# Another order of columns in the three-part matmuls of a whole-model kernel, and six offsets for the weights' split tiles

## The reference

```
x = x + gate * hybrid_mixer(modulate(x))    # gated linear attention and three-way sparse attention
x = x + gate * swiglu(modulate(x))          # dense feed-forward
x = x + gate * mamba2_mixer(modulate(x))    # state-space layer
x = x + gate * moe_ffn(modulate(x))         # 8 experts, the best 2 for each token
x = rmsnorm(x, final_norm)
for layer in range(2):                      # dilated attention beside block-sparse attention
    x = hybrid_layer(x, c, cos, sin, ...)
```

## Time and profile before

| | |
|---|---|
| median of 3 runs | 2075.34 us (2073.47 to 2078.24) |
| the profiled execution | 2075.21 us, span 2073.4 us |
| TensorE matmuls, weight loads | 95% and 79% of the span busy |
| VectorE, ScalarE | 83% and 64% |
| mean granted TensorE clock | 0.982 of 2.4 GHz |
| moved by DMA | 560 MB, 270 GB/s on the mean |

### The profile page before, as it was taken

One profiled execution on the slowest core, in us unless ns is written; L12 is line 12 of the kernel. 1 busy time (PEld: TensorE's weight loads), 2 busy tenths in 40 slices (PEclk: granted clock), 3 DMA queues, 4 the chain that ended last, 5 costly groups with the idle time before them and its releaser, 6 DMA issues.

```text
span 2073.4 us, 28446 instructions
## 1 busy us (share of the span) xinstructions
PE 1975.6 (95%) x10316; PEld 1644.3 (79%) x10316; DVE 1725.3 (83%) x2440; ACT 1328.1 (64%) x1977; POOL 0.2 (0%) x4
## 2 busy tenths in 40 slices
PE   6998999989989999999999999999999998999997
PEld 5777889978877788788888878888888876767785
DVE  7798878768776698989989898998989988785764
ACT  4353534355564587788788787888878774554543
POOL 0000000000000000000000000000000000000000
PEclk9999999999999999999999999999999999999999
DMA  9856689846332298999999999999989994672630
GB/s 378 300 170 234 229 301 327 287 142 207 116 111 82 91 382 325 359 334 382 366 351 365 329 368 345 374 352 340 371 325 377 380 354 158 222 247 68 217 122 21
DMA packets 154211, 560.19 MB, mean 270 GB/s; under 512 B 17232, under 2 KB 17488, under 8 KB 153936
## 3 DMA queue, kind: packets, MB, share of 16 engines
q1 hardware_dynamic: 154064, 558.29, 74.1%
HBM read 557.18 MB, written 1.05 MB: 269 GB/s over the span
## 4 chain that ended last, share of the span: by engine, by line
PE 78%; DVE 12%; ACT 5%; issue 3%; DMA 2%; DVEq 0%; SPq 0%; ACTq 0%
PE ps L527 22%; PE ps L529 22%; PE ps L528 22%; PE ps L533 10%; DVE spl L516 3%; PE ps L537 3%; DVE macc L580 2%; ACT sph L504 2%; DMA ring<-in_hyb_w_in 1%; DVE arena L2169 1%; DMA ring<-in_dense_down 1%; ACT arena L771 1%; ACT arena L2135 0%; DVE hL L884 0%; ACT ps L890 0%
## 5 line engine op out<-in xcount | busy, mean ns | idle before, releaser
L504 ACT ACTIVATE sph<-ring 128x1024 fp32r<-128x1024 f32 x906 | 949.2, 1059 | 517.0 <-PE ps L529 332.8
L516 DVE TENSOR_TENSOR spl<-ring,sph 128x1024 fp32r<-128x1024 f32 x906 | 1078.2, 1219 | 241.5 <-ACT sph L504 229.0
L527 PE MATMUL ps<-sph,hH 128*128 128x512 f32 (+1 forms) x1296 | 522.6, 403 | 1.4 <-DVE hL L884 1.3
L529 PE MATMUL ps<-sph,hL 128*128 128x512 f32 (+1 forms) x1296 | 507.8, 392 | 0.0
L528 PE MATMUL ps<-spl,hH 128*128 128x512 f32 (+1 forms) x1296 | 506.9, 391 | 0.0
L529 PEld LDWEIGHTS ps<-sph,hL 128*128 128x128 f32 x1296 | 245.5, 189 | 52.6
L527 PEld LDWEIGHTS ps<-sph,hH 128*128 128x128 f32 x1296 | 246.4, 190 | 51.3 <-issue 3.8
L528 PEld LDWEIGHTS ps<-spl,hH 128*128 128x128 f32 x1296 | 246.4, 190 | 48.4 <-issue 1.0
L527 PE MATMUL ps<-sph,rH 128*128 128x512 f32 x664 | 269.1, 405 | 5.9 <-ACT arena L3123 2.3
L529 PE MATMUL ps<-sph,rL 128*128 128x512 f32 x664 | 259.9, 391 | 0.0
L528 PE MATMUL ps<-spl,rH 128*128 128x512 f32 x664 | 259.4, 391 | 0.0
(11 more groups left out here) (317 smaller groups left out, 1754.4 us busy)
## 6 DMA issues: line engine op xcount, KB each, us to landing
ring<-in_moe_gu SPq DMA_DIRECT2D x448, 512.0 KB, 5.4
ring<-in_moe_down SPq DMA_DIRECT2D x224, 512.0 KB, 5.3
ring<-in_mod SPq DMA_DIRECT2D x144, 512.0 KB, 5.0
ring<-in_w_in SPq DMA_DIRECT2D x64, 512.0 KB, 4.5
ring<-in_dense_gu SPq DMA_DIRECT2D x44, 512.0 KB, 5.3
ring<-in_ssm_w_in SPq DMA_DIRECT2D x40, 512.0 KB, 4.2
ring<-in_dense_down SPq DMA_DIRECT2D x22, 512.0 KB, 5.4
ring<-in_hyb_w_in SPq DMA_DIRECT2D x20, 512.0 KB, 5.9
```

What stands on the lines that cost most here:

```text
L504: a.activation(k.high[m % SPLITS][:, 0:w], raw[:, 0:w], ACT.Copy).then_inc(k.S.half_rounded, 1)
L516: v.tensor_tensor(k.low[m % SPLITS][:, 0:w], raw[:, 0:w], k.high[m % SPLITS][:, 0:w], ALU.subtract).then_inc(*k.tick(k.S.half_split, f"hal ...
L527: pe.matmul(out, a[0], b[0], start=start, stop=False, skip_group_check=True)
L529: return pe.matmul(out, a[1], b[0], start=False, stop=stop, skip_group_check=True)
```

## The change

The moving operand of `mm3`, and its result in PSUM in the same way, are walked in another order of columns when their number is a multiple of 256. The columns are seen as two halves of n groups of 16; the groups are taken from the last to the first, and from each the 16 columns of the first half and then those of the second. The result lands at the same places as before. The pairs `sph`, `spl` are set apart by pads, so that pair i begins LEADS[i] float32 columns (0, 64, 128, 192, 320, 448 bytes) further modulo 512 than `hH`. The pads make 448 bytes, which also shift all tiles behind them (`macc`, `mods`, `ring`, `arena` and others); a reserve for descriptors in SBUF is made smaller to have the room (no transfer here is started from GpSimd).

```diff
+LEADS = (0, 16, 32, 48, 80, 112)
...
-        self.high = [sb(f"sph{i}", [128, QUARTER], F32R) for i in range(SPLITS)]
-        self.low = [sb(f"spl{i}", [128, QUARTER], F32R) for i in range(SPLITS)]
+        self.high, self.low = [], []
+        for i, lead in enumerate(LEADS):
+            if (lead - LEADS[i - 1] if i else lead) % 128:
+                sb(f"pad{i}", [128, (lead - LEADS[i - 1] if i else lead) % 128])
+            self.high.append(sb(f"sph{i}", [128, QUARTER], F32R))
+            self.low.append(sb(f"spl{i}", [128, QUARTER], F32R))
...
+def paced(ap):
+
+    return ap.rearrange("p (j n i) -> p n j i", j=2, i=16)[:, ::-1] if ap.shape[1] % 256 == 0 else ap
+
+
 def mm3(pe, out, a, b, start, stop):
-    pe.matmul(out, a[0], b[0], start=start, stop=False, skip_group_check=True)
-    pe.matmul(out, a[0], b[1], start=False, stop=False, skip_group_check=True)
-    return pe.matmul(out, a[1], b[0], start=False, stop=stop, skip_group_check=True)
+    out, high, low = paced(out), paced(b[0]), paced(b[1])
+    pe.matmul(out, a[0], high, start=start, stop=False, skip_group_check=True)
+    pe.matmul(out, a[0], low, start=False, stop=False, skip_group_check=True)
+    return pe.matmul(out, a[1], high, start=False, stop=stop, skip_group_check=True)
...
-    nc = _bacc.Bacc("TRN2", target_bir_lowering=False, num_devices=1)
+    nc = _bacc.Bacc("TRN2", target_bir_lowering=False, num_devices=1, dynamic_dma_scratch_size=1024)
```

## The result

The changed kernel takes 2079.28 us (median of 20 runs, 2072.85 to 2085.06), the kernel before 2074.28 us in as many runs on the same chips (2068.16 to 2079.80). The ratio is 1.0024 with a 95% interval of 1.0014 to 1.0034: 5 us slower, between 2.9 and 7.1. The prediction said 50 us faster. Of its four cases none came out as told. The change is a little slower; the sign given for rival (c) did show (distances that depend on the buffer, over 230 ns in three of six, see the table further down), but not its 13 ns.

The account below looks back on a forecast made before the run. The distance between `mm3`'s starts was taken to bound the kernel. Saving 8.5 ns each, 27.1 us in the experts' stage and 22.8 outside, gave 2075.2 - 49.9 = 2025 us; own range 2000 to 2055, whole range 2000 to 2100.

Parts of the forecast that it names:

- rival (c): In `mm3`, streams kept at one place in some buffers: 13 ns a matmul lost, 2118 to 2162 us; chance 0.17.
- the prediction's own sum: Whole kernel: `mm3` matmuls by stage times 8.5 ns, 27.1 us kept in the experts' stage, 22.8 outside, together 49.9.
- The 71%: Outside the experts' stage: share of `mm3`'s start distances that the chain of waits holds, 463 of 648 us; 22.8 us saved.
- The surplus of 13 ns: In `mm3` at full clock: 13.3 ns per matmul over its columns' time, read as two read streams of TensorE meeting.
- Part (2): Six places of the pairs in SBUF: the distance of the two streams differs by buffer; some can still meet.
- rival (b): In `mm3`, the surplus is the swap of the weights, not a meeting: saving zero, 2075 us; chance 0.16.
- Part (3): Tiles behind the pads lie elsewhere modulo 512 bytes; costed at nothing, VectorE's half of a split staying at 1219 ns.
- the price of one matmul: In `mm3`: a saving of 8.5 ns per matmul, chosen between a saving of 11.3 and a loss of 13 ns.
- (d): In `mm3`, 32 address jumps per 512-column matmul at 0.83 ns each cost 26.7 ns: 2178 us; chance 0.07.
- the ring: SBUF places modulo 512 bytes, where the moving read and the weights' load were said to meet; one load is one turn.
- The DMA limit: Experts' stage: DMA engines 0.95 busy, floor 931 us, so 8 tenths of 33.9 us kept, 27.1 us.
- Meeting at the same place: In `mm3`, the moving read and the next weights' load meet in SBUF and cost the faster one some slots.

Follow-up runs that it names:

- f3_lead16: Kernel before, order kept; stationary quarter blocks put 16 columns further in their tiles where 256 tokens move: 2070.68 us against 2076.31, ratio 0.9972.
- f4_lead48: Changed kernel with all six pairs 48 columns off instead of six different places: 2069.93 us against 2076.60 for the kernel before, ratio 0.9973.
- m5_line: Model's work left out, series of 40 matmuls: repeated columns with a walking load (4 columns 218.7 ns), and plain fp32 in four orders (429.1 ns a row).
- The grids: Five kernels without the model's work, only series of 40 equal matmuls, each with its own weights' load; distances count, their time says nothing.
- m1_grid: Model's work left out, series of 40 matmuls: several column orders, each at offsets 0 to 112; 512 columns upwards at offset 0 took 226.7 ns.
- f1_order: Changed kernel with the new column order alone, all six pairs at offset 0: 2088.22 us against 2074.53 for the kernel before, ratio 1.0064.
- f5_lead64: Changed kernel with all six pairs 64 columns off instead of six different places: 2086.09 us, ratio 1.0048 to the kernel before.
- f2_leads: Changed kernel with the six places alone, columns read upwards as before: 2085.37 us, ratio 1.0056 to the kernel before.
- f6_both: Changed kernel, new order for 512 columns only, all pairs 48 columns off, stationary blocks 32 further where 256 tokens move: 2072.52 us against 2075.14, ratio 0.9983.
- m4_stay: Model's work left out, series of 40 matmuls with one or both reads staying at one place: 16 repeated columns 243.3 ns, 4 repeated 218.7, load staying too.

## Why the prediction was wrong

**What held.** The distance of `mm3`'s starts sets the time: put into the prediction's own sum (3987 x d512 + 0.71 x (1845 x d512 + 1920 x d256)), the measured changes of +1.8 and -2.6 ns give 7.2 + 2.4 - 3.5 = 6 us, and 5 were measured. For the gainful side too it comes close: f3_lead16 -7 (measured -5.8), f4_lead48 -6 (-5.6). So the counts do for small changes. The 71% was never tested by itself, and where the distances grow more the sum is too high (below). The surplus of 13 ns is there only at the full rate of reading; plain fp32 in every order and the low clock confirm it. (The reading of the earlier trace rows was 2 ns low: those twelve rows start 429 to 431 ns apart, not 427, as in m5_line. That leaves 2.6 ns over and makes the bound 10.7 instead of 11.3.) Part (2) does act by the relation of two reads, since shifting either one changes the distance and shifting both doesn't, so rival (b), the fixed cost, is out. Part (3), the tiles behind the pads, cost nothing that shows: 1221 ns a split against 1219.

**The step that failed** is the price of one matmul: "the streams keep their distance and don't meet", a saving of 8.5 ns. Measured: a loss of 1.8 for 512 columns, a saving of 2.6 for 256. Three things in it were wrong.

First, I took the surplus of 13.3 ns as the cost of meetings that could be avoided. The grids found no order and no offset below 226.7 ns for fp32r reads of 512 different columns, and 226.7 is what the old layout has: every tile at offset 0, read upwards. I had bounded the saving by the half-rate rows, and no row of a full-rate read stood at that bound. The 256 form had room, from 120.0 to 113.3, and by the offset alone.

Second, the steps of 16 columns were costed at nothing by themselves in the forecast. At offset 0 they take 230 to 233 ns (paced) or 240 (halves upwards) against 226.7, by the read alone. It is the order of magnitude of rival (c)'s 13 ns, by something nearer to (d), a cost of jumps, though not (d)'s: it doesn't grow in step with their number (16 runs 236.6, 32 runs 233.4, 64 runs 251.3, 128 runs 246.6) and is gone at runs of 64 columns, or with runs of 16 at offset 48. The rule behind (d), in the Trainium skill's "Advanced Engine Details and Errata", PSUM Cachelines, is about the write: with the write alone in steps of 16 the distance stayed 226.7, so runs that short cost nothing in PSUM here; the read's jumps were the dear ones.

Third, the ring has 64 columns (256 bytes), not 512 bytes. So the leads of 80 and 112 are 16 and 48 again, and the six places are four. The table sets beside each other what the paced series of m1_grid give for the six pairs and what the changed kernel shows (ns, by the pair of the load or read):

```
lead of the pair        0      16      32      48      80     112    mean
grid, 512 paced     230.0   228.4   228.4   226.7   228.2   226.7   228.1
kernel, 512         231.4   228.3   229.2   228.4   230.6   230.7   229.8
grid, 256 paced     120.6   117.4   116.6   116.7   117.4   116.7   117.6
kernel, 256         122.2   119.1   116.0   117.3   119.4   116.5   118.5
```

(With the weights stationary a lead of n is an offset of -n, so the grid's row is read from the other side.) For 512 columns lead 0 is the worst in both, and 48 is within 0.1 ns of the best; for 256 lead 0 is the worst and 32 the best. The pairs at 80 and 112 are 2.4 and 4.0 ns above the grid for 512 columns. Before the change, with all at one place, the six pairs already differ by 1.5 ns (227.2 to 228.7), and a layout can settle at two distances (f4_lead48); what part of the 4 ns these make was not found.

**The rule weighed against the rows.** The Trainium skill's "TensorE: Matmul & The Clock Gate", Part 2, has the load of weights take no read bandwidth from the matmul. It would have given 2075, closer than my number. Yet the rows speak against it as it stands: shifting only the load by 16 columns moves the distance from 226.7 to 233.4. That it is read bandwidth which is lost there, no run shows. The rule's number was nearer because the old offset happened to be the best one for 512 columns, and because the gain in the 256 form takes back a third of the loss (3.5 of 9.6 us in the sum).

**The DMA limit** (8 tenths of the gain kept in the experts' stage) stays untested, since no distance fell there by more than half a ns: the changed kernel's stage moved 355 GB/s. In f4_lead48 the mean there fell from 227.7 to 227.2 ns, 2 us over 3984 matmuls, and the stage was no shorter (977.5 us against 977.1).

**What stays open.** The mechanism below the rule. "Meeting at the same place" is refuted (4 repeated columns take 218.7 ns wherever the load stands, 16 take 243.3). Why the period is 256 bytes, why a shorter load is no help, and why one layout settles at 230.0 or 233.4 (paced at 0), or at 226.7 or 236.0 (paced at 48), was not found.

Where the distances of 512 columns grow most, the sum is too high: f1_order and f5_lead64 have some +3.5 and +0.8 ns, which make 20 us, and measured were 13.3 and 10.0; f2_leads has 14 against 11.6. The experts' stage shows a part of the reason. There the distances of f1_order add up to 13 us more than before, but the stage (the 158th to the 822nd quarter block) is only 9.2 us longer, because the distances over 300 ns, in which TensorE waits, fell from 43.5 to 38.2 us in sum; in f5_lead64, 8.6 us longer, to 36.9. A TensorE that goes slower waits less. For the small changes the sum holds within 2 us, but for f6_both (-6 against -3.5, within its interval).

**The best version** is f3_lead16 or f4_lead48, 0.28% and 0.27% faster than the kernel before, not told apart by their intervals. f3_lead16 leaves the order of the read as it was.

## What to carry to other kernels

Where TensorE reads fp32r at full rate, let the moving operand run through at least 64 columns (256 bytes) without a jump, and treat the offset of moving and stationary operand modulo 256 bytes as a parameter: here it is worth up to 8 ns of 227 and 7 of 120. Check it in the whole kernel: the paced order at offset 48, 226.7 ns in the grid, stood at 236 in a part of f4_lead48. A surplus over columns by clock is no saving until some series shows a distance without it: a kernel of 40 equal matmuls for each layout gives the answer for all of them at once, ahead of any edit of the real kernel. And an edit with two halves is best taken apart: here each half alone was slower than both.

## What the runs showed of the hardware that I had not expected

- fp32r matmuls of 512 columns with a load each are 226.7 to 234.6 ns apart upwards, by the offset of the moving read to the load modulo 256 bytes; of 256 columns 113.3 to 120.0. bf16 in the same series is at 215.8 to 215.9 in the three layouts tried.
- The read's runs count: 246.6 ns in steps of 4, 251.3 of 8, 230.0 or 233.4 of 16, 236.6 of 32, 226.7 of 64 and 128 (paced, offset 0). In steps of 16 the same order in the write alone cost nothing. Single columns read downwards take 233.3.
- One layout can stay at either of two distances, with no wait and at full clock: 226.7 and 236.0 ns in one execution of f4_lead48.
- The recorded length of an fp32r load is 188, 134, 109 and 89 ns for 128, 64, 32 and 8 columns, and the distance of 512-column matmuls 226.7, 230.1, 231.7 and 231.0: the shorter load doesn't bring them closer.
- A moving read that repeats 4 or 8 columns takes 218.7 and 217.8 ns, less than any read of different columns; one that repeats 16 takes up to 246.7 (m4_stay, at column 48), more than most.
- The best offset isn't the same for the two lengths: of the multiples of 16 upwards it is 0 for 512 columns (48 is the worst, 233.4) and 48 for 256 (113.3; 0 is the worst, 120.0).
- The nine profiled executions of whole kernels spent between 48 and 83 us at the low clock. By the mean granted clock recorded with each execution, a thousandth less (some 4 us at the low clock) goes with 1.1 us more within one kernel's runs, so those 35 us stand for some 10 us, as much as the differences told here; only several runs show them. Set to one clock in this way, f3_lead16 and f4_lead48 are 4.9 and 5.2 us faster (an estimate from the executions on record).
